# Prompt attention: value rows, index pairs and picks placed singly on the steps

## The reference

```
def indexer_topk(q_i, w_i, q_pos, k_i, topk):
    s = jnp.einsum('bqhd,bkd->bqhk', q_i, k_i) * IDX_DIM ** -0.5
    score = jnp.einsum('bqhk,bqh->bqk', relu(s), w_i)
    score = where(k_pos <= q_pos, score, NEG_INF)
    return lax.top_k(score, topk)[1]          # prompt: 132 of up to 528 keys

# branch A and B of the prompt, for blocks of 128 queries, 8 heads each
p = softmax(where(allowed, q @ k * scale, NEG_INF));  o = p @ v

# branch B of the decode requests: each of 64 query tokens has its own 256 picked rows
k_sel = gather_selected(pool_k, page_table, k_b, idx, past_len)
v_sel = gather_selected(pool_v, page_table, v_b, idx, past_len)
o = softmax(q . k_sel) . v_sel
```

## Time and profile before

| | us |
|---|---|
| time before, median of 3 | 1731.18 (1729.77 to 1731.21) |
| the profiled execution | 1730.1 |
| its span | 1728.3 |
| TensorE busy | 1620.8 (94%) |
| VectorE busy | 870.2 (50%) |
| ScalarE busy | 419.2 (24%) |
| GpSimd busy | 316.4 (18%) |

### The profile page before, as it was taken

One profiled execution on the slowest core, in us unless ns is written; L12 is line 12 of the kernel. 1 busy time (PEld: TensorE's weight loads), 2 busy tenths in 40 slices (PEclk: granted clock), 3 DMA queues, 4 the chain that ended last, 5 costly groups with the idle time before them and its releaser, 6 DMA issues.

```text
span 1728.3 us, 21560 instructions
## 1 busy us (share of the span) xinstructions
PE 1620.8 (94%) x8540; PEld 985.8 (57%) x8540; DVE 870.2 (50%) x1640; ACT 419.2 (24%) x1112; POOL 316.4 (18%) x332
## 2 busy tenths in 40 slices
PE   5999989999999799998878899999999999989998
PEld 3654455446776465665455566447777777744443
DVE  3447799999993878774773343222322323210011
ACT  2131312001004455553446531001111111100010
POOL 2100000010004757760446730000000000000000
PEclk8899998999999899997779999999999999999999
DMA  6521203142406778767446845312122122111100
GB/s 191 187 75 62 89 30 128 64 180 93 150 36 226 254 273 328 288 239 217 114 131 185 310 121 196 103 37 72 49 79 68 49 74 73 49 61 49 66 23 32
DMA packets 87541, 218.36 MB, mean 126 GB/s; under 512 B 13320, under 2 KB 37264, under 8 KB 83440
## 3 DMA queue, kind: packets, MB, share of 16 engines
q0 software_dynamic: 26864, 116.66, 19.8%
q1 hardware_dynamic: 60578, 100.33, 17.7%
HBM read 199.99 MB, written 16.84 MB: 125 GB/s over the span
## 4 chain that ended last, share of the span: by engine, by line
PE 82%; DVE 9%; DMA 3%; POOL 2%; issue 2%; ACT 2%; DVEq 0%; SPq 0%; ACTq 0%
PE PS L2186 13%; PE PS L647 13%; PE PS L2231 11%; PE PS L2214 7%; PE PS L698 7%; PE PS L2163 4%; PE PS L766 3%; PE PS L1116 2%; PE PS L1050 2%; PE PS L1704 2%; POOL mem L1943 2%; PE PS L2140 2%; PE PS L1584 2%; PE PS L2603 1%; PE PS L1686 1%
## 5 line engine op out<-in xcount | busy, mean ns | idle before, releaser
L647 PE MATMUL PS<-mem 128*128 128x512 f32 (+3 forms) x580 | 232.7, 557 | 0.0
L2186 PE MATMUL PS<-mem 128*128 128x376 f32 x704 | 231.7, 481 | 0.0
L2231 PE MATMUL PS<-mem 128*128 128x512 f32 (+1 forms) x440 | 190.7, 595 | 1.4 <-DVE mem L2410 1.4
L2186 PEld LDWEIGHTS PS<-mem 128*128 128x128 f32 x704 | 131.0, 189 | 79.3
L647 PEld LDWEIGHTS PS<-mem 128*128 128x128 f32 (+1 forms) x580 | 99.8, 185 | 119.1 <-issue 118.9
L1943 POOL DMA_INDIRECT mem<-in_cache_dsa_k,mem x128 | 136.8, 1069 | 147.2 <-issue 135.5
L1943 POOL DMA_INDIRECT mem<-in_cache_dsa_v,mem x128 | 123.3, 964 | 143.4 <-PE PS L1686 107.5
L2231 PEld LDWEIGHTS PS<-mem 128*128 128x128 f32 (+1 forms) x440 | 80.1, 182 | 111.4 <-issue 109.8
L2214 PE MATMUL PS<-mem 128*128 128x216 f32 x704 | 135.8, 345 | 0.0
L2214 PEld LDWEIGHTS PS<-mem 128*128 128x128 f32 x704 | 129.2, 189 | 10.7
L2391 DVE TENSOR_SCALAR mem<-mem 128x528 f32<-128x528 f32 x22 | 12.2, 555 | 238.7 <-ACT mem L2294 238.7
(11 more groups left out here) (332 smaller groups left out, 2033.0 us busy)
## 6 DMA issues: line engine op xcount, KB each, us to landing
mem<-in_w_in SPq DMA_DIRECT2D x10, 2048.0 KB, 8.2
mem<-in_w_ffn_g SPq DMA_DIRECT2D x11, 1024.0 KB, 5.3
mem<-in_w_ffn_u SPq DMA_DIRECT2D x11, 1024.0 KB, 5.3
mem<-in_w_ffn_d SPq DMA_DIRECT2D x10, 1024.0 KB, 5.0
tmp_gates<-mem SPq DMA_DIRECT2D x16, 296.0 KB, 2.1
mem<-tmp_gates SPq DMA_DIRECT2D x16, 296.0 KB, 3.7
mem<-in_w_o SPq DMA_DIRECT2D x2, 2048.0 KB, 10.6
mem<-in_x_prompt SPq DMA_DIRECT2D x6, 512.0 KB, 12.3
```

The costliest lines, as they stand in the source:

```text
L647: ins = pe.matmul(PS[0:n, b[bank], out_at:out_at + width], left[:, k, cols], w[:, k, at:at + width], start=k == 0, stop=k == k_range - 1)
L2186: pe.matmul(PS[:, 3 * (f % 2) + j, 0:UP_A], w[:, k, :], h2T[:, k, 0:UP_A], start=k == 0, stop=k == KD - 1)
L2231: return pe.matmul(PS[0:TW[m], (5 * n + m) % 8, :], upT[:, f, token_cols(m)], w[:, i, :], start=f == 0, stop=f == NF - 1)
```

## The change

The order of the tiles is not touched. Three tables and one bank change:

- `v_cost`: every step but those of b2 and b3 has weight 7, b2 has 2 and b3 has 0. By `v_upto` that is 2 or 3 rows on each of steps 0 to 27, and one each on steps 28, 30 and 31.
- `index_at`: one index pair a step, tile 2 on steps 0 to 3 and tile 3 on steps 10 to 13.
- `pick_at`: tile 2's picks on steps 4 to 9, in 12 parts, and tile 3's on steps 14 to 21, in 16 parts. `pick` gets the number of parts as an argument.
- Both quads of a4 take banks 6 and 7, and the wait of the first value row goes.

```
-        pick_at = {pair_no["a", host, i]: (m, i) for host, m in ((0, 2), (1, 3)) for i in range(4)}
-        v_cost = [{("a", 4): 0, ("b", 4): 4, ("a", 0): 6, ("b", 0): 3, ("a", 1): 6, ("b", 1): 5, ("a", 2): 7,
-                   ("b", 2): 4, ("a", 3): 8, ("b", 3): 5}[x[0:2]] for x in pairs_p]
+        pick_at = {n: (2, n - 4, 6) for n in range(4, 10)} | {n: (3, n - 14, 8) for n in range(14, 22)}
+        v_cost = [{("b", 2): 2, ("b", 3): 0}.get(x[0:2], 7) for x in pairs_p]
...
-        index_at = {}
-        for hosts, m in ((tile("a", 4, quads), 2), (tile("b", 4, quads), 3)):
-            for j, host in enumerate(hosts):
-                index_at[pair_no[host]] = [("i", m, 2 * j), ("i", m, 2 * j + 1)]
+        index_at = {n: [("i", 2, n)] for n in range(4)} | {n: [("i", 3, n - 10)] for n in range(10, 14)}
...
             if g[1] == 4:
-                banks_p[g] = [0, 1] if g == ("a", 4, 1) else [6, 7]
+                banks_p[g] = [6, 7]
...
                 q = x[0]
                 g, i = q // 4, q % 4
-                if q == 0:
-                    pe.wait_ge(sem("masked"), upto("masked", ("a", 4, 1)))
                 if i == 0 and g:
                     pe.wait_ge(sem("v_sums_out"), upto("v_sums_out", g - 1))
                 pe.wait_ge(sem(f"rows_in{q % 5}"), upto(f"rows_in{q % 5}", "v", q))
...
                     dve.tensor_scalar(p, p, st[:, 3:4], None, ALU.mult).then_inc(
                         sem("normed_b"), tick("normed_b", g))
-            def pick(m, h):
+            def pick(m, part, parts):
                 keys = KEYS[m]
                 rounds = TOPK_P // 8 + 1
                 all_s = score_acc[:, 0:4 + keys]
-                for _ in range(rounds * h // H, rounds * (h + 1) // H):
+                for _ in range(rounds * part // parts, rounds * (part + 1) // parts):
                     link(dve.max(top8_p, all_s))
                     link(dve.match_replace(all_s, top8_p, all_s, TAKEN))
-                if h == H - 1:
+                if part == parts - 1:
                     mask = mask_of[m]
                     link(dve.tensor_scalar(mask[:, 0:keys], score_acc[:, 4:4 + keys], -2e38, NEG,
...
                     mask_scores(g)
                 if n in pick_at:
-                    m, i = pick_at[n]
-                    pick(m, 2 * i)
+                    m, i, steps = pick_at[n]
+                    pick(m, 2 * i, 2 * steps)
...
                 if n in pick_at:
-                    m, i = pick_at[n]
-                    pick(m, 2 * i + 1)
+                    m, i, steps = pick_at[n]
+                    pick(m, 2 * i + 1, 2 * steps)
```

## The result

| | before | changed |
|---|---|---|
| median, us | 1730.47 (4 runs) | 1717.5 (4 runs) |
| the profiled span, us | 1728.3 | 1716.1 |
| mean granted clock | 0.956 | 0.963 |

The ratio is 0.993 with a 95% interval of 0.9913 to 0.9947: faster by 0.7%, 13 us of the 25 that were forecast. The change works where it was expected to work, in two of the three stretches, and loses in the third.

What follows compares the result with a forecast made beforehand. Engines waiting for each other bound steps 0 to 13, GpSimd's gathers steps 14 to 27, TensorE steps 28 to 35. Gains of 17 us up to step 28 and 8 after it sum to 25, giving 1706 us, range 1696 to 1722.

Steps and rivals of the forecast that it cites:

- Steps 0 to 13: First stretch of the prompt attention: step 14 would start at 894 us, 16 us earlier than before.
- The first gather: Sign in GpSimd's timeline: the first gather after the first five rows comes near 814 us, not 827.5.
- idle time and clock would cancel: Steps 0 to 13: TensorE's idle time, about 8 us against 23.3 before, was let cancel with the granted clock.
- Steps 28 to 35: Last stretch: TensorE sheds 10 rows, 3 turns and a stop for copied sums; gain 8 us, ends 6 and 9.
- Steps 14 to 27: Middle stretch: 70 us by gathers plus 2 for stops and transfers; step 28 at 966, a gain of 17 us.
- a lead of five rows: Steps 14 to 27: five buffers let GpSimd run five rows ahead, so row 34 is issued 3 us before step 14.
- The price of the stops: TensorE's waits for copied sums: 1.8 us each in steps 5, 7, 9; 2 us with crowded transfers in steps 14 to 27.
- the rival of a partly low clock: Clock low in half of the early steps, or stops for copied sums add up: 1714 to 1718 us; chance 0.20.
- The gathers alone as a floor: Rival: gathers set the pace from the first step, step 28 at 958.5, gain 32, 1699 us; chance 0.10.
- The slow rival of a low clock: Low clock level throughout steps 0 to 13: step 14 at 931, step 28 at 1003, about 1743 us; chance 0.09.
- The port: Rival: VectorE's work locks GpSimd's port, a row takes 4.4 us, some 70 us slower; chance 0.02.
- All on the path: The whole 25 us counts, 17 up to step 28 and 8 after, since the next stage waits for this one's end.

Runs made afterwards that it cites:

- the kernel with the picks alone: Index pairs and picks as in the changed kernel, value rows dealt out as in the kernel before; 1713.4 us, ratio 0.9897 to the kernel before.
- the one with two rows a step but the old picks: Changed kernel with two value rows on each of steps 0 to 31, index pairs and picks where they were before; 1714.6 us, ratio 0.99.
- half the gathers: Changed kernel without the first of the two gathers of each value row from row 5 on; 1709.8 us, ratio 0.9875.
- both cures: Changed kernel with ScalarE's copy of the value sums ahead of exp and one gather a row from row 5 on; 1688.8 us, ratio 0.9751.
- the kernel with the copy first: Changed kernel with ScalarE's copy of the value sums ahead of the step's exp, not behind it; 1708.7 us, ratio 0.9866.
- The kernel that takes four rows back to the end: Changed kernel with two rows a step, none on steps 22 and 26, and ScalarE's copy ahead of exp; 1692.0 us, ratio 0.9765.

## Why the prediction was right or wrong

- **Steps 0 to 13: right.** Step 14 was forecast 83.2 us after step 0 and came after 83.9. The first gather came 3.2 us after step 0 (3.1 forecast). The reason given holds too: the kernel with the picks alone has the gain, and the one with two rows a step but the old picks (90.8 us) shows the picks as a bound by themselves. That idle time and clock would cancel was a guess that came out, and partly luck: TensorE idled 11.9 us where some 8 were taken (8.5 of it in stops for the copy, not the 5.4 of three at 1.8), and its busy time fell by 12.4, to 72.0 us at a clock of 0.85 where 84.4 at 0.71 were counted.
- **Steps 28 to 35: right.** 8 us forecast, 7.3 measured.
- **Steps 14 to 27: wrong, and this is the step that failed.** The prediction said "row 34 is issued then, and row 60 ... 26 x 2.5 = 65 us later", with step 28 some 70 us after step 14, and took 2 us for stops and transfers. Row 60 did come 65 us after row 34 (899.37 and 964.34). But row 34 was issued 2.6 us after step 14 began and not 3 us before it: five buffers were taken for a lead of five rows. A stop of TensorE stops GpSimd too; from 816 to 899 the 29 rows took 83.4 us where 72.5 would do, 6.8 of the difference in one pause before 878.09. That is 5.6 us. From row 60 to step 28 lay 12.9 us and not 8.6, 4.3 more. Together 9.9, against the 2 us that were allowed (and the 70.6 that the sum gives was rounded to 70). The path was wrong too, not only its length. Gathers from end to end are a fair reading of the kernel before, where gathers and their landings have 59% of the middle's chain of waits, but the chain of the changed kernel has none before 949 and does not pass through row 60. It passes through row 56, whose landing took 7.01 us where 4.1 was taken, then through TensorE's own work, at a clock of 0.67 from 965 to 970, and through one more stop for the copy, 1.94 us ahead of row 60.
- **The price of the stops was mis-sized.** They were named (steps 5, 7 and 9, 1.8 us each), but in the middle they shared 2 us with the crowded transfers, and are 10.4 us. The experiments make of it two bounds of like height: with the stops cut to 4.7 us the middle is still 82.0 (gathers and their landings), with half the gathers still 75.0 (stops of 12.0), with both cures 64.6. The new weights make both: 61 rows must be gathered ahead of step 28, and the last row of a group of four shares a step with the first of the next in eight of steps 5 to 27.
- **The rivals.** The time, 1717.5, lies where the rival of a partly low clock had it (1714 to 1718, "or the stops for copied sums add up"), but that rival put the loss ahead of step 14, where there was none. The gathers alone as a floor (step 28 147.7 us after step 0) is what the kernel with the copy first comes near, at 156.0. The slow rival of a low clock did not come: 0.85. The port did not either: in the middle, beside 48.2 us of VectorE's work, a gather took 946 ns in the median and 1415 at most. By the rule of the Trainium skill (SBUF — State Buffer, "SBUF: two separate sides") a locked port would have stretched them; these picks and masks do not show it.
- **"All on the path" held only at one end.** 10 rows that leave the late stretch save 7 us there, and were counted as free ahead of step 28, where each is 2.5 us of GpSimd. The kernel that takes four rows back to the end is faster by 2 to 4 us.

## What to carry to other kernels

When a table deals work out over steps, price each unit on every engine that it passes: a value row costs TensorE half a microsecond and GpSimd 2.5, so the place with room on TensorE can be the wrong one. Buffers are not a lead; a queue that is fed back from its user loses what the user loses, so look for where the user stops. And align units that end a group with the step, which here cut the stops from 18.8 to 2.2 us, or put the copy that closes the group ahead of work that waits for another engine, which cut them to 7.0. An engine without a pause is not yet the bound: look whether the chain of waits goes through it.

## What the runs showed of the hardware

With the same matmuls in the middle, TensorE was busy 64.4 us at a granted clock of 0.90 (changed, 16 us idle), 63.9 at 0.92 (copy first, 18 us idle) and 57.7 at 1.00 (both cures, 7 us idle). So in the third kernel a shorter wait was paid twice, as idle time and as clock; between the first two, idle time and clock do not go together. The Trainium skill (TensorE: Matmul & The Clock Gate, Part 1: The HAM clock gate) says that activity releases the clock; the third kernel agrees, and the first two do not decide it. The clock's drop behind a stop is seen in two windows of the changed kernel (busy us by engine, clock, DMA share): from 865 TensorE works 3.07 of 5 us with a stop in it, and from 870 it is busy all the time at half the clock. The third window is the crowd on the DMA engines at 960:

```profile
865.00:870.00 5.00, 3.07 (x45) 2.20 (x44) 4.41 (x16) 3.08 (x11) 3.69 (x4) 0.93 0.68 191
870.00:875.00 5.00, 5.00 (x22) 4.53 (x22) 0.64 (x2) 0.65 (x3) 0.99 (x2) 0.50 0.48 146
960.00:965.00 5.00, 2.87 (x38) 1.76 (x40) 0.39 (x2) 0.92 (x3) 3.78 (x5) 0.65 1.04 388
```
